# Attention over the prompt with the keys on partitions: one inversion of all softmax sums, and the division moved to GpSimd in the output projection

## The chip, the cores and the metric

The kernel runs as one program on one NeuronCore of a Trainium2 chip. The metric is the device time of one execution in microseconds, the median of several runs. The engines are TensorE (PE, with its weight loads as PEld), VectorE (DVE), ScalarE (ACT), GpSimd (POOL) and the DMA queues, the most of them fed by SyncE (SP).

## What is computed

One encoder layer for 1024 prompt tokens (8 tiles of 128 rows) and 128 sample tokens (a ninth tile). The part that the change touches is the token mixer's attention over the prompt, 8 heads, chunk-causal with chunks of 64, and what follows it:

```
proj = x @ w_in                       # cq, ckv, kr, gates gb, gc, gv
q  = rms(cq) @ w_uq                   # 8 heads x (64 + 32 rotary)
kv = rms(ckv) @ w_ukv                 # 8 heads x (64 key + 64 value)
s  = (qn.kn + qr.kr) * 96**-0.5, masked where key chunk > query chunk
p  = softmax(s);  attn = p @ v
y  = concat(attn, gb * conv3(gc * gv)) @ w_out
x  = layer_norm(alpha * x + y)        # then cross attention, LN, experts, LN
```

The sample tokens attend over a cache of 512 latents each, cross attention and a routed layer of 32 experts follow for all nine tiles.

## The kernel before

The five engines run hand-written programs side by side, each in its own order, and hand over by semaphores. PSUM is four tiles of two banks each, T[0], T[1], M[0], M[1] (128 x 1024 f32). Matrix products that must be exact but cheap use operands split in a rounded high part (ACT casts to fp32r, "high") and a low part (the difference, `take_low`, line 1629, on DVE), and three products of such parts. Others use plain f32 operands, for which the trace shows two matmul records each.

**Stages, in order of time.** Memory keys and values; the projections of nine tiles (lines 734 to 775); the attention over the prompt (PE lines 778 to 828); the attention of the sample tokens over the cache (PE lines 831 to 903, eight batches); the output projection with the first layer norm (PE lines 906 to 956, called "projection with w_out" here); cross attention; routing and experts.

**The prompt attention.** The values of all heads are eight f32 products (L782), copied out by ACT (L1333). Then per head: eight transposes turn the queries (L791), ACT copies them out with the scale (L1337); two f32 products give the keys (L795), DVE copies them (L1698). Then for eight query tiles, in the order ORDER = (2, 4, 6, 7, 5, 3, 1, 0), with the queries on partitions: scores in f32 (L806), DVE writes the mask (L1704) and takes the row maximum (L1706), ACT takes exp with the row sum accumulated (L1341), PE transposes the probabilities (L689), DVE copies them (L1719), PE multiplies them with the values in f32, 64 columns at a time (L816), and DVE scales the 128x64 result by the inverse of the row sum (L1721, L1713). SP loads each head's queries and key weights two heads ahead (L495, L496).

**The cache attention.** PE transposes the sample queries and the weights (L835, L838); ACT scales the first into qTs (L1346), DVE copies the second (L1731). Eight batches follow, and in each of them ACT and DVE split one 128-row chunk of w_out (L1376, L1629). ACT waits for all chunks of w_out (line 1366, `win_lo_in`) before the first batch's exp (L1370). GpSimd begins the convolution of tiles 0 to 3 in this stage.

**The projection with w_out.** For each tile t: GpSimd has the convolution's rows (`convolve`, lines 2143 to 2158: three multiplications in one group L2151, then L2154, L2156, L2158, all 128x512); PE turns the eight 128-column chunks of attention and convolution (`turn_mix`, L918); ACT casts the turned rows to the high part (L1388); DVE takes the low part (`mix_low`, L1770); PE runs 48 matmuls of 128x512 (L911); DVE adds the residual and takes mean and variance (`add_first`: L1755, L1757, L1758, L1761); GpSimd gives the inverse deviation (`deviation`: L2119, L2121); DVE normalises (`norm_rows`: L1765, L1768); SP stores the rows. The orders that matter, each engine's own:

```
DVE:  mix_low(0); for t in 0..7: mix_low(t+1), norm_rows(t-1), add_first(t)
POOL: convolve(0..3); for t in 0..7: deviation(t), convolve(t+4)
PE:   turn_mix(0); for t in 0..8: turn_mix(t+1), product(t)
```

ACT issues the 25 loads of the sample tile's convolution behind its cast of tile 5 (L1393, L1394). SP loads tile t's convolution inputs (`load_conv`, L519) with two buffers, and the residual rows (`load_x`, L528).

## Time and profile before

| | us |
|---|---|
| median of 3 runs | 1743.56 |
| lowest, highest | 1738.17, 1748.22 |
| profiled execution, its own time | 1737.2 |
| its span in the trace | 1735.4 |
| PE busy in the span | 1612.0 (93%) |
| DVE, ACT, POOL busy | 993.6, 751.8, 249.4 |
| mean granted TensorE clock | 0.976 |

Busy time of PE is the union of matmul records, and these overlap: a record of 128x512 lasts longer than the distance to the next. In a timeline a line stands for one instruction or for several of a kind, with its start, its length, and in brackets the idle time before it and who ended that.

### The profile page before, as it was taken

The numbers are of one execution on the slowest core, as the hardware profiler recorded it, in microseconds if no ns is written. First come the engines' busy times: TensorE is split into PE (matmuls) and PEld (weight loads), VectorE is DVE, ScalarE is ACT, GpSimd is POOL, SyncE is SP. The second block draws the span as 40 slices with busy tenths as digits, with TensorE's granted clock in tenths as the row PEclk, the third lists the DMA queues.
The fourth block names the chain that finished last, engine by engine and source line by source line (L and its number), as shares of the span: only waits on it lengthen the run. The fifth ranks groups of instructions, "written<-read, shape, count | busy, mean of one in ns | idle before, by whom it ended". The sixth has DMA issues, their size and how long they took to land.

```text
span 1735.4 us, 21728 instructions
## 1 busy us (share of the span) xinstructions
PE 1612.0 (93%) x8282; PEld 1292.7 (74%) x8282; DVE 993.6 (57%) x1347; ACT 751.8 (43%) x1062; POOL 249.4 (14%) x210
## 2 busy tenths in 40 slices
PE   8999999799998899999999998999999999999966
PEld 4578877466766688999877777788888888888852
DVE  1410111366665456422344447889988889889936
ACT  2311111332335202222332113588778778788834
POOL 0000000000007173000021110111111121111104
PEclk9999999999999999999999897999999999999988
DMA  9510111700002354300054445799999999999967
GB/s 356 216 62 29 61 53 47 240 20 20 10 12 98 146 192 172 134 25 13 22 184 149 143 136 216 258 376 379 379 383 387 376 389 385 390 383 377 363 231 299
DMA packets 134295, 351.77 MB, mean 203 GB/s; under 512 B 24498, under 2 KB 27186, under 8 KB 128708
## 3 DMA queue, kind: packets, MB, share of 16 engines
q1 hardware_dynamic: 124084, 330.69, 51.6%
q0 software_dynamic: 9216, 18.89, 2.8%
q10 hardware_dynamic: 912, 1.05, 0.2%
q8 instruction: 56, 0.92, 0.2%
q14 instruction: 27, 0.22, 0.0%
HBM read 322.19 MB, written 43.15 MB: 211 GB/s over the span
## 4 chain that ended last, share of the span: by engine, by line
PE 58%; DMA 20%; DVE 13%; ACT 4%; issue 3%; SPq 1%; POOL 0%; DVEq 0%; POOLq 0%; ACTq 0%
DMA beside<-in_w_exp_up 18%; PE M L911 11%; DVE rounded L1629 10%; PE T L753 6%; PE M L744 5%; PE M L816 3%; PE T L689 3%; PE M L1159 3%; PE T L806 3%; PE M L689 2%; PE T L970 2%; ACT rounded L1517 2%; PE T L972 2%; PE T L971 2%; PE M L999 2%
## 5 line engine op out<-in xcount | busy, mean ns | idle before, releaser
L1159 PE MATMUL M<-rounded 128*128 128x512 f32 x2304 | 548.9, 395 | 11.2 <-DVE conv_w_rows L1960 5.6
L1629 DVE TENSOR_TENSOR rounded<-beside,rounded 128x1024 fp32r<-128x1024 f32 (+2 forms) x394 | 468.0, 1234 | 114.3 <-ACT rounded L1517 56.6
L1159 PEld LDWEIGHTS M<-rounded 128*128 128x128 f32 x2304 | 429.1, 189 | 105.6 <-issue 15.0
L1517 ACT CAST rounded<-beside 128x1024 fp32r<-128x1024 f32 x256 | 259.2, 1050 | 94.9 <-DMA beside<-in_w_exp_up 88.1
L911 PE MATMUL M<-rounded 128*128 128x512 f32 x864 | 216.5, 407 | 5.2 <-DVE logits L1852 2.3
L911 PEld LDWEIGHTS M<-rounded 128*128 128x128 f32 x864 | 164.9, 195 | 43.6 <-issue 7.9
L1527 ACT CAST rounded<-beside 128x1024 fp32r<-128x1024 f32 x128 | 125.3, 1048 | 19.5 <-DMA beside<-in_w_exp_down 17.2
L2201 POOL DMA_INDIRECT expert_rows<-beside,route_out x32 | 44.4, 1389 | 380.1 <-ACT beside L1558 360.6
L1341 ACT ACTIVATE arena<-T,negmax 128x384 f32<-128x384 f32 (+3 forms) x64 | 47.4, 740 | 114.6 <-DVE negmax L1706 114.6
L1629 DVE TENSOR_TENSOR rounded<-T,rounded 128x512 fp32r<-128x512 f32 (+1 forms) x82 | 81.7, 1000 | 26.2 <-ACT rounded L1401 18.2
L689 PE MATMUL T<-tables,arena 128*128 128x128 f32 x572 | 77.8, 284 | 17.3 <-DMA arena<-in_mem_prompt 6.7
L689 PEld LDWEIGHTS T<-tables,arena 128*128 128x128 f32 x572 | 68.1, 146 | 32.9 <-issue 11.5
L806 PE MATMUL T<-arena 96*128 96x384 f32 (+3 forms) x192 | 71.8, 489 | 10.8 <-issue 10.8
L816 PEld LDWEIGHTS M<-arena 128*128 128x128 f32 x576 | 71.8, 192 | 10.3 <-issue 7.7
L744 PE MATMUL M<-rounded,x_high 128*128 128x416 f32 (+1 forms) x270 | 70.4, 374 | 6.6 <-DVE x_low L1629 6.6
L970 PE MATMUL T<-rounded 128*128 128x256 f32 x256 | 73.1, 285 | 2.4 <-issue 2.4
L816 PE MATMUL M<-arena 128*128 x576 | 72.5, 271 | 0.7
L971 PE MATMUL T<-rounded 128*128 128x256 f32 x256 | 72.4, 283 | 0.0
L972 PE MATMUL T<-rounded 128*128 128x256 f32 x256 | 72.4, 283 | 0.0
L2194 POOL DMA_INDIRECT beside<-x_rows,route_tok x32 | 52.2, 1632 | 135.6 <-PE T L1200 115.3
L753 PE MATMUL T<-rounded,x_high 128*128 128x512 f32 x270 | 65.4, 394 | 0.0
L753 PEld LDWEIGHTS T<-rounded,x_high 128*128 128x128 f32 x270 | 50.7, 188 | 11.7
(302 smaller groups left out, 2107.5 us busy)
## 6 DMA issues: line engine op xcount, KB each, us to landing
beside<-in_w_exp_gate SPq DMA_DIRECT2D x64, 1024.0 KB, 8.5
beside<-in_w_exp_up SPq DMA_DIRECT2D x64, 1024.0 KB, 11.3
beside<-in_w_exp_down SPq DMA_DIRECT2D x32, 2048.0 KB, 11.6
arena<-x_rows SPq DMA_DIRECT2D x27, 512.0 KB, 4.0
x_rows<-arena SPq DMA_DIRECT2D x18, 512.0 KB, 3.0
arena<-expert_rows SPq DMA_DIRECT2D x9, 1024.0 KB, 12.8
arena<-in_x_prompt SPq DMA_DIRECT2D x16, 512.0 KB, 3.9
arena<-in_cache_mem_k SPq DMA_DIRECT2D x8, 1024.0 KB, 5.8
```

The source lines that it names most:

```text
L689: got = nc.tensor.transpose(out[:, k * P:(k + 1) * P] if width == P else out[0:width, k * P:(k + 1) * P], rows[:, k * width:(k + 1) * widt ...
L744: got = nc.tensor.matmul(M[u][:, at:at + c1 - c0], x[:, k * P:(k + 1) * P], part[k][:, c0:c1], start=(k == 0 and part is w_in_high and x i ...
L753: got = nc.tensor.matmul(T[u][:, c:c + CW], x[:, k * P:(k + 1) * P], part[k][:, GC + c:GC + c + CW], start=(k == 0 and part is w_in_high a ...
L806: got = nc.tensor.matmul(T[n % 2][:, c:c1], qT[u][0:HW, i * P:(i + 1) * P], kT[u][0:HW, c:c1], start=True, stop=True)
L816: got = nc.tensor.matmul(o, prT[n % 2][:, c, :], value[:, c, ds(h * DV, DV)], start=(c == 0), stop=(c == i))
L911: got = nc.tensor.matmul(out[:, c:c + 512], x[k], part(k)[:, c:c + 512], start=(k == 0 and x is hi and part is high), stop=(k == KT - 1 an ...
L970: nc.tensor.matmul(out, high(k)[:, d * P:(d + 1) * P], x1T[:, 0, k], start=(k == 0), stop=False)
L971: nc.tensor.matmul(out, high(k)[:, d * P:(d + 1) * P], x1T[:, 1, k], start=False, stop=False)
L1159: got = nc.tensor.matmul(out, x[xs], (high, low)[ws](w)[:, c:c + 512], start=(first and n == 0), stop=(last and n == 2))
L1517: nc.scalar.copy(high(c), w_raw[c // 4][:, c % 4, :]).then_inc(gu_high, 1)
L1527: nc.scalar.copy(high(8 + c), w_raw[2][:, c, :]).then_inc(down_high, 1)
L1629: return nc.vector.tensor_tensor(out, x, highs.bitcast(f32), ALU.subtract)
```

## The change

In the prompt attention the keys stand on the partitions of the scores, so that the probabilities come out already in the form in which they multiply the values, and their transposes go. The row maximum is needed before the exp and per column, so it becomes part of the product: a first, rougher set of scores ("lead scores": high parts alone, queries on partitions, the 12 pieces LEADS of up to 512 columns) gives each query's maximum on DVE (`largest`); it is written as a 97th column beside the query's 96 numbers, turned with them, and meets a row of ones in the keys. Scores and values are then three products of high and low parts each. The sum of the probabilities comes from ones beside the values: 64 more output rows of the same matmul. The mask is a matmul of one row. ACT takes each exp twice (f32 and rounded), GpSimd subtracts them for the low part. Scores of one head run beside lead scores of the next.

The output of the attention, attnT, is already turned, so `turn_mix` turns only the convolution's four chunks. It is not yet divided: the sums of each head go to DRAM, come back as 64 rows, are inverted once by DVE in the cache stage (b == 3), go to DRAM again, and are loaded spread over partitions, tile by tile (`load_shares`, two DMAs each, tiles 0 and 1 by SP, 2 to 7 by ACT). GpSimd multiplies attnT by them (`divide_by_sums`).

```diff
 PE, prompt attention
+            for n in range(PT * H):
+                h, j = divmod(n, PT)
+                scores(n)
+                if n > 1:
+                    weigh_values(n - 2)
+                if h + 1 < H:
+                    if j == 0:
+                        keys(h + 1)
+                    if 1 <= j <= 4:
+                        for c in range(3 * j - 3, 3 * j):
+                            lead_scores(h + 1, c)
+                    if j == 5:
+                        turn_with_max(h + 1)
+                if j == 6 and h + 2 < H:
+                    turn_queries(h + 2)
...
+            def lead_scores(h, c):
...
+                    pe.wait_ge(negmax_ready, MAXES * h + c - 1)
...
+            def scores(n):
...
+                if n > 1:
+                    pe.wait_ge(exp_done, n - 1)
...
+                for c0, c1 in by_banks(j):
+                    for m, (k, q) in enumerate(((kT_hi, qa_hi), (kT_hi, qa_lo), (kT_lo, qa_hi))):
...
 ACT, prompt attention
+            def exponentials(n):
+                j = n % PT
+                act.wait_ge(s_ps, n + 1)
+                if n > 1:
+                    act.wait_ge(p_ready, n - 1)
+                if n > 2:
+                    act.wait_ge(o_ps, n - 2)
+                nc.scalar.activation(p_raw[n % 2][:, 0:D - j * P], T[n % 2][:, j * P:], ACT.Exp)
+                nc.scalar.activation(p_hi[n % 3][:, 0:D - j * P], T[n % 2][:, j * P:], ACT.Exp).then_inc(exp_done, 1)
...
+            act.wait_ge(sums_out, 16 * H)
 DVE, prompt attention
+            for h in range(H):
+                if h + 1 < H:
+                    keys_low(h + 1)
+                if h > 0:
+                    context(h - 1, 1)
+                if h + 1 < H:
+                    for c in range(len(LEADS)):
+                        largest(h + 1, c)
+                    larger_part(h + 1)
+                context(h, 0)
+                if h + 1 < H:
+                    scaled_low(h + 1)
+            context(H - 1, 1)
 SP, after the prompt attention
+            store_sums(H - 1)
+            load_conv(0)
+            load_conv(1)
+            sp.wait_ge(sums_out, 16 * H)
+            sp.dma_start(r_sums[0:64, :], sums_dram.rearrange("h (t c) -> (h t) c", t=PT)).then_inc(sums_out, 16)
+            for k in range(4):
+                sp.dma_start(w_out_raw[k], w_out_rows[:, k, :]).then_inc(win_lo_in, 16)
...
 DVE, cache attention
+                if b == 3:
+                    dve.wait_ge(sums_out, 16 * (H + 1))
+                    nc.vector.reciprocal(r_sums[0:64, :], r_sums[0:64, :]).then_inc(o_done, 1)
 PE, turn_mix
-                if t < PT:
-                    transposes(T[u], attn[:, t, :], 4)
-                transposes(T[u][:, 512:], conv_rows[t % 4], 4).then_inc(rowsT_ps, 1)
+                transposes(T[u][:, 512:], conv_rows[t % 3], 4).then_inc(rowsT_ps, 1)
 ACT, projection with w_out
             for t in range(NT):
                 u = t % 2
-                act.wait_ge(rowsT_ps, t + 1)
+                if t < PT:
+                    act.wait_ge(o_done, 2 * H + 1 + t + 1)
+                if t + 2 < PT:
+                    load_shares(act, t + 2)
                 if t > 1:
                     act.wait_ge(product_ps, t - 1)
-                if t < PT:
-                    nc.scalar.copy(rows_hi[u], T[u][:, :]).then_inc(rows_high, 1)
+                nc.scalar.copy(rows_hi[u][:, 0:512].rearrange("p (k c) -> p k c", k=4), attnT[:, :, t * P:(t + 1) * P] if t < PT else mixTs)
+                act.wait_ge(rowsT_ps, t + 1)
+                nc.scalar.copy(rows_hi[u][:, 512:], T[u][:, 512:]).then_inc(rows_high, 1)
 DVE, mix_low
-                if t < PT:
-                    take_low(rows_lo[u], T[u][:, :], rows_hi[u]).then_inc(rows_low, 1)
...
+                k, left = (x[u][:, 0:512].rearrange("p (k c) -> p k c", k=4) for x in (rows_lo, rows_hi))
+                take_low(k, attnT[:, :, t * P:(t + 1) * P] if t < PT else mixTs, left)
+                take_low(rows_lo[u][:, 512:], T[u][:, 512:], rows_hi[u][:, 512:]).then_inc(rows_low, 1)
 POOL
+            for n in range(PT * H):
+                w, hi, lo, raw = D - (n % PT) * P, p_hi[n % 3], p_lo[n % 3], p_raw[n % 2]
+                pool.wait_ge(exp_done, n + 1)
+                nc.gpsimd.tensor_tensor(lo[:, 0:w], raw[:, 0:w], hi[:, 0:w].bitcast(f32), ALU.subtract).then_inc(p_ready, 1)
...
+            def divide_by_sums(t):
+                pool.wait_ge(share_in[t % 2], 32 * (H // 2) + 32 * (t // 2 + 1))
+                rows = attnT[:, :, t * P:(t + 1) * P]
+                nc.gpsimd.tensor_tensor(rows, rows, shares[t and 2 - t % 2], ALU.mult).then_inc(o_done, 1)
+
-            for t in range(4):
+            for t in range(3):
                 convolve(t)
+            divide_by_sums(0)
             for t in range(PT):
+                if t + 1 < PT:
+                    divide_by_sums(t + 1)
                 deviation(t, t % 2)
-                if t + 4 < NT:
-                    convolve(t + 4)
+                if t + 3 < NT:
+                    convolve(t + 3)
             deviation(PT, 0)
```

Around these: every SBUF area of the stage has a new place; the convolution's rows have three buffers instead of four, so that three tiles are convolved ahead; the first two heads' queries are loaded before the last tile's projection is stored; four of the eight chunks of w_out, the sample queries and the sample latents are loaded behind the prompt attention; the shift of the second layer norm is loaded later, and the load of w_ukv waits for the memory values' store. DVE prepares mask rows, rows of ones and zeros and the low part of the rotary keys once (memsets and two subtractions of 32x1024), and ACT copies the rotary keys twice. The DVE order of the projection with w_out stands as it was.

## Rows read from the trace of the kernel before

**Rows 1.** Busy time by engine, prompt attention and projection with w_out (columns: stretch, length, engines, clock, DMA).
```profile
329.60:525.60 196.00, 181.60 (x1146) 138.74 (x1147) 131.41 (x327) 60.33 (x135) 0.00 (x0) 1.00 0.13 40
588.38:694.40 106.02, 105.95 (x500) 88.00 (x500) 61.24 (x63) 15.40 (x17) 52.10 (x46) 1.00 0.55 200
```

**Rows 2.** Timeline, the first scores of heads 0 and 7.
```profile
329.64 1.96 PE L806 MATMUL T<-arena 96*128 96x384 f32 x6 [1.36 <-issue]
...
504.32 1.96 PE L806 MATMUL T<-arena 96*128 96x384 f32 x6 [1.35 <-issue]
```

**Rows 3.** Groups by shape, 340 to 700 us, TensorE (busy us, mean ns of one).
```profile
L911 PE MATMUL M<-rounded 128*128 128x512 f32 x432 | 100.7, 392 | 1.6 <-ACT rounded L1388 1.6
L816 PE MATMUL M<-arena 128*128 x562 | 70.9, 271 | 0.7
```

**Rows 4.** Timeline of TensorE, fp32r matmuls of 256 columns, and one head's keys.
```profile
706.16 0.28 PE L970 MATMUL T<-rounded 128*128 128x256 f32 x1
...
706.52 0.28 PE L970 MATMUL T<-rounded 128*128 128x256 f32 x1
...
351.16 1.93 PE L795 MATMUL M<-arena 128*64 128x512 f32 x4
```

**Rows 5.** Groups by shape, 340 to 700 us, DVE and ACT.
```profile
L1706 DVE TENSOR_REDUCE negmax<-T 128x1 f32<-128x512 f32 x8 | 5.5, 691 | 0.3
L1706 DVE TENSOR_REDUCE negmax<-T 128x1 f32<-128x256 f32 x8 | 3.4, 424 | 0.3
L1341 ACT ACTIVATE arena<-T,negmax 128x1024 f32<-128x1024 f32 x7 | 7.8, 1113 | 9.5 <-DVE negmax L1706 9.5
L1341 ACT ACTIVATE arena<-T,negmax 128x128 f32<-128x128 f32 x8 | 2.9, 367 | 13.2 <-DVE negmax L1706 13.2
L1353 ACT COPY arena<-T 128x512 f32<-128x512 f32 x8 | 4.6, 569 | 2.3 <-PE T L854 2.3
```

**Rows 6.** Groups by shape, GpSimd, whole span.
```profile
L2151 POOL TENSOR_TENSOR arena<-arena,conv_w_rows 128x512 f32<-128x512 f32 x27 | 42.1, 1588 | 10.3 <-DMA arena<-gate_rows 10.3
L2174 POOL TENSOR_TENSOR rounded<-beside,rounded 128x1024 fp32r<-128x1024 f32 x9 | 21.3, 2372 | 179.7 <-ACT rounded L1467 179.7
```

**Rows 7.** Timeline, hand-over of tiles in the projection with w_out.
```profile
599.65 1.22 DVE L1755 SCALAR_TENSOR_TENSOR arena<-arena,M 128x1024 f32<-128x1024 f32 x1 [10.24 <-PE M L911]
...
602.34 0.21 DVE L1761 BATCH_NORM_AGGREGATE moments<-stats 128x2 f32<-128x12 f32 x1
...
603.05 0.57 POOL L2121 TENSOR_TENSOR rstd<-moments,minus_half 128x1 f32<-128x1 f32 x1
...
614.25 1.17 DVE L1629 TENSOR_TENSOR rounded<-T,rounded 128x1024 fp32r<-128x1024 f32 x1
...
615.34 1.28 DVE L1765 SCALAR_TENSOR_TENSOR arena<-arena,moments 128x1024 f32<-128x1024 f32 x1
616.65 1.28 DVE L1768 SCALAR_TENSOR_TENSOR arena<-arena,rstd 128x1024 f32<-128x1024 f32 x1
617.77 3.83 POOL L2151 TENSOR_TENSOR arena<-arena,conv_w_rows 128x512 f32<-128x512 f32 x3 [1.97 <-DMA arena<-gate_rows]
...
624.41 1.29 POOL L2158 TENSOR_TENSOR arena<-arena 128x512 f32<-128x512 f32 x1
```

**Rows 8.** The line of the DMAs that ACT issues (ns min, median, max of one issue).
```profile
L1393 ACTq DMA_DIRECT2D arena<-u_rows_sample x24: 366/442/734, 637.2 to 648.5; - x24
```

**Rows 9.** Timeline before the first head: ACT's start, and TensorE after an idle stretch.
```profile
314.76 1.04 ACT L1330 COPY arena<-arena 32x1024 f32<-32x1024 f32 x1 [3.75 <-DMA q_rows<-arena]
...
323.91 1.94 PE L791 MATMUL M<-tables,arena 128*96 128x128 f32 x8 [5.71 <-DMA arena<-in_w_ukv]
325.78 2.50 PE L795 MATMUL M<-arena 128*64 128x512 f32 x4
```

**Rows 10.** The cache stage's first exp, and the loads of w_out (KB, us to landing).
```profile
535.70 0.70 ACT L1370 ACTIVATE arena<-M,negmax 128x528 f32<-128x528 f32 x1 [2.21 <-DVE negmax L1740]
...
below<-in_w_out SPq DMA_DIRECT2D x8, 512.0 KB, 6.7
```

More of the change, by code:

```diff
@@ new lines, in values @@
+            def values(i, dst):
+                got = nc.tensor.matmul(dst, latT[:, i * P:(i + 1) * P], w_ukv[:, :, DN:], start=True, stop=True)
+                got.then_inc(value_ps, 1)
+            VALUE_IN = [T[0][:, 512:], T[1][:, 512:], M[1][:, 0:512], M[1][:, 512:]]
+            turn_queries(0)
+            pe.wait_ge(win_lo_in, 16)
+            for i in range(4):
+                values(i, VALUE_IN[i])
+            keys(0)
+            for c in range(len(LEADS)):
+                lead_scores(0, c)
+                if c % 3 == 2:
+                    i = 4 + c // 3
+                    pe.wait_ge(value_ready, i - 3)
+                    values(i, VALUE_IN[i - 4])
@@ L1329, in _ @@
             act.wait_ge(q_rows, 2 + NT)
[L1330 to L1342 removed]
+            act.wait_ge(conv_ps, NT)
@@ L1852, in add_logits @@
                 nc.vector.tensor_tensor(logits[:, t, :], M[t % 2][:, 0:NG + NE], b_router[:, :], ALU.add).then_inc(logits_done, 1)
-            def then(ins):
-                ins.then_inc(dve_step, step.next())
-                dve.wait_ge(dve_step, step.value())
             def wide(x, *shape):
```

470 lines of the change are left out of this document (284 added, 186 removed).

## Prediction

> **What bounds the kernel now.** I read the busy time by stage first: in the prompt attention PE is busy 181.6 of 196.0 us, in the projection with w_out 105.95 of 106.0 [rows 1]. Both are TensorE's, so time is won there only by less work for PE, and lost where PE is made to wait. Then I read the timeline of one head and of one tile of the projection, for who waits for whom, and the groups by shape for prices. A head takes (504.32 - 329.64) / 7 = 24.95 us now [rows 2], a tile of the projection 106.0 / 9 = 11.78 us [rows 1].
>
> **Prices.** An fp32r matmul of 512 columns takes 100.7 / 432 = 0.233 us, one of 256 columns a third of 0.36 = 0.12 us [rows 3, 4]. For 384 columns I take 0.18, between them. For narrower ones no row shows fp32r; L816, with 64 columns and a weight load of 128, takes 70.9 / 562 = 0.126 a record [rows 3], so weights bound it: I take 0.12, also for the transposes and the mask matmuls (64 columns). The keys of a head are four records in 1.93 us [rows 4], 1.8 without the last one's tail, unchanged. A result can be read some 0.16 us after its matmul's slot (392 less 233 ns).
>
> **A head after, if PE never waits.** The causal half is 12 pieces: six of 512 columns, two of 384, two of 256, two of 128, 1.40 + 0.36 + 0.48 = 2.24 us a set. Scores are three sets, values three, lead scores one: 15.7. Sixteen masks 1.9, keys 1.8, sixteen transposes 1.9: 21.3 us. The other engines are below that. ACT: sixteen exps, from 1.11 us at 1024 columns to 0.37 at 128 [rows 5], mean 0.74: 11.8, and six copies of 512 columns at 0.57 [rows 5]: 15.2. DVE: reductions 6 x 0.69 + 2 x 0.56 + 2 x 0.42 + 2 x 0.29 [rows 5] = 6.7, and eight instructions of 512 columns at 0.69: 12.2. POOL: 4608 columns; 2.37 us at 1024 [rows 6] and 1.29 at 512 [rows 7] give 9.7 + 8 x 0.2 = 11.3.
>
> **But PE waits for the maxima.** The lead scores go through the two banks of M[0] and are issued three in a row; PE's order is strict. The third needs the first's maximum: 0.16 us, then 0.56 to 0.69 of reduction, 0.1 back, less the second's own 0.23. That is 0.60, 0.74 and 0.60 us at j = 2, 3, 4. At j = 1 it is worse: DVE stands behind the low parts of the keys and `context(h-1, 1)`, whose two copies (1.3 us) start only when the last values of the previous head are done, right before the first lead scores. With scores(0) at 0 I get: values and keys to 3.6, scores(1) and values to 5.3, first lead scores to 6.1; DVE's copies end at 6.9, the first maximum at 7.6, the third lead at 7.7: 1.6 us. The sum is 21.3 + 3.6 = **24.9, say 25.0 us a head: what it is now**. The expected gain of about 3.6 us a head goes into the maxima. ACT lags nowhere in that walk: its keys, queries and scaled copies end before PE asks.
>
> **The start.** The first scores are at 329.6 now. After, ACT starts as now at 314.76 [rows 9], since the same stores are waited for; two rotary copies take 2.0. DVE then has memsets of single rows and two 32x1024 subtractions: I take 7 us (5 to 8; no row shows a memset of one row of 1024), the low parts of four value tiles 2.9, keys 1.3, then twelve maxima with four more value tiles between them 9.9, and turning and scaling 2.8: scores at 340.8. The early load of the first heads saves the 5.7 us for which PE waits for key weights now [rows 9], but DVE sets the start, so it gives nothing. Head 0 has no predecessor to finish: 23.0. Six more at 25.0. The last head has no lead scores and is bound by ACT's two exps and GpSimd's subtraction in turns (two raw buffers): I walk it to 15.2, and 1.9 more for values and copies. The attention ends at 340.8 + 23 + 150 + 17.1 = 530.9 against 525.5: **+5.4**.
>
> **The cache stage.** ACT now waits for the last sums' store before it writes qTs, which takes their place: some 2 us behind the end, +0.6 on PE's start, since the present start waits for its own copies 2.7 us. Four chunks of w_out are loaded behind two `load_conv` and the sums: issued by 5.1 to 6.5 us after the end, landing 6.7 us later at worst [rows 10]; the first exp stands 10.2 us after the end now (535.70), so ACT loses 0 to 2.5, I take 1.5. What is queued behind it there is the whole stage. Inversion (one instruction of 64x128), its round trip through DRAM and the loads of shares 0 and 1 end 30 us before they are needed. The sample's queries and latents land under head 7, the second norm's shift and the first heads' queries under other work: nothing. The projection with w_out starts at **+7.3** (5.4 + 0.6 + 1.5, less 0.2 for transposes).
>
> **The projection with w_out is where it is lost.** DVE's order is mix_low(t+1), norm_rows(t-1), add_first(t). mix_low(t+1) needs ACT's high part, and that now needs divide_by_sums(t+1). GpSimd does this behind deviation(t-1) **and** convolve(t+2). deviation(t-1) needs the variance, the end of add_first(t-1). So from one variance V(t-1) to the next everything is in a row, and PE's product, 11.2 us, lies beside it:
> - to the end of deviation: 603.62 - 602.55 = 1.1 [rows 7];
> - convolve: 617.77 to 625.70, 7.95 [rows 7];
> - divide: 128x512 on GpSimd, 1.29 [rows 7];
> - ACT issues two DMAs first, for rows 2 to 5: 2 x 0.44 = 0.9 [rows 8];
> - two copies of 512 columns, 1.1 [rows 5];
> - mix_low in two halves, 1.25 (one of 1024 takes 1.17) [rows 7];
> - norm_rows, 615.34 to 617.93: 2.6 [rows 7];
> - add_first, 599.65 to 602.55: 2.9 [rows 7];
> - five hand-overs, 0.25.
>
> That is 19.3 us (18.4 without the DMAs) against 11.78, for six cycles (the convolutions 3 to 8 that stand in the loop): 4 x 19.3 + 2 x 18.4 = 114. Product 7 starts 11.15 + 0.1 + 2.9 + 114 - 5.5 = 122.7 us after product 0, against 7 x 11.78 = 82.5: +40.2. PE then idles about 8 us in each cycle. After 5.7 idle us the clock was below full: the keys took 2.50 instead of 1.93 and the transposes before them 1.94 instead of 1.0 [rows 4, 9]. In the cycles a slower product is hidden; before product 7 it is not: +1.5. Products 7 and 8 keep half a microsecond each from their missing transposes: -0.9. **+40.8** in this stage.
>
> GpSimd's own price has two values. Multiplications of the convolution took 1.28 us when alone (3.83 for three) and 1.59 in the mean [rows 6, 7]; with the mean the cycle would be about 1.05 longer, the stage +6. I take the lower: in the new cycle DVE waits while GpSimd convolves. The Trainium skill, "SBUF — State Buffer", section "Who interferes with whom", says that a DVE instruction with two SBUF inputs contends with a GpSimd instruction that reads SBUF. The longer multiplications here stand beside DVE's norm_rows, so the trace agrees; by that rule the convolutions run undisturbed and the sum keeps the lower price.
>
> **Sum.** +7.3 + 40.8 = +48. Everything behind (cross attention, experts, whose weight loads are released by the cross attention's end) is shifted as a whole. Against the profiled execution, 1737.2, that is 1785; that execution lies 6.4 below the median of the runs, 1743.6, to which I add the same: **1792**.
>
> **Rivals.**
> - A: the attention runs at PE's sum, 21.3 a head, because maxima are hidden after all (DVE overlaps neighbours, PE's issue runs ahead). For it: DVE is busy only half of a head. Against it: the wait on `negmax_ready` stands in PE's own queue, two leads behind. 7 x 3.6 = 25 less: 1767.
> - B, the other side: the division does not hold DVE back, and the projection stays PE's. Its place is divide(t+1) against add_first(t): it decides where GpSimd's 10.3 us (deviation, convolve, divide) no longer start at the variance, that is if divisions run a tile further ahead than their order says. For it: GpSimd's sum of 10.3 is under 11.78. Against it: the order of its loop. The stage would be 4 us shorter: 1743.6 + 7.3 - 4 = 1747, no difference; with A as well 1722, faster.
> - C: heads are slower (27 us), from fp32r matmuls of 128 columns dearer than 0.12 (12 more of them a head at up to 0.2), ACT's DMA issues, or contention: +14 and +6: 1812.
>
> **How the numbers follow.** My case 0.65 (its own range 1780 to 1804), A 0.13, C 0.10, B alone 0.05, B with A 0.07. Half a per cent, 8.7 us, is what counts as a difference. Slower: 0.65 + 0.13 + 0.10 = 0.88, same 0.05, faster 0.07. The range leaves out B (0.12) and the edges of C: 1758 (A, with 3 us less of memsets and cycles 1 us shorter) to 1815.
>
> **What would show it.** In the profile after: first scores near 341; heads 25 us apart, with four idle stretches of PE in each ended by DVE's maxima, the longest behind `context`; last context near 531; first matmul of the w_out product near 596; then products 19 us apart, PE idle some 8 us before each, ended by DVE's low part, that by ACT, that by GpSimd's division, for products 2 to 7; the ninth right behind the eighth. Products 12 us apart would make me wrong on the larger term; heads at 21 or 27 us on the smaller one.

## The result, and the profile after

| | before | after |
|---|---|---|
| median, us (four runs each) | 1741.09 | 1862.62 |
| lowest, highest | 1738.17, 1748.22 | 1855.76, 1868.28 |
| profiled execution, span | 1737.2, 1735.4 | 1859.32, 1857.5 |
| mean granted TensorE clock | 0.976 | 0.938 |

The ratio is 1.069 (95% interval 1.0636 to 1.0744). The changed kernel is slower, as forecast, but by 122 us instead of 48, and outside the range. The profile shows where: the first product with w_out starts at 669.33 instead of 588.38 [rows 1], 81 us late where 7.3 were forecast, and the projection adds 41, as forecast. Behind it both traces run equally long: 1041 us from the end of the ninth product to the end of the program.

Busy time by engine of the four stretches, columns as in [rows 1]: attention, cache stage, products 0 to 6, and from product 7 to the start of the next stage.
```profile
349.16:600.54 251.38, 237.50 (x927) 172.01 (x928) 86.26 (x151) 96.91 (x169) 90.42 (x64) 0.83 0.05 15
600.54:669.33 68.79, 52.39 (x292) 37.62 (x290) 28.36 (x44) 32.15 (x61) 26.98 (x22) 0.93 0.29 99
669.33:790.94 121.61, 92.04 (x364) 72.64 (x365) 37.40 (x49) 8.73 (x16) 59.01 (x55) 0.89 0.43 144
790.94:819.00 28.06, 25.23 (x113) 20.64 (x113) 22.03 (x24) 10.03 (x10) 3.36 (x4) 0.95 0.59 225
```

TensorE's clock in the attention was 1.00 before; now its mean is 0.83, and 0.89 in the projection. PE is busy 237.5 of 251.4 us, so the attention is still PE's: it is the same engine with dearer work, not another engine. The first scores of heads 0 and 7 in the timeline of TensorE answer to [rows 2]:

```profile
349.19 0.94 PE L878 MATMUL T<-rounded 97*128 97x512 f32 x3 [0.74 <-ACT x_high L1438]
...
580.61 0.86 PE L878 MATMUL T<-rounded 97*128 97x512 f32 x3
```

(580.61 - 349.19) / 7 = 33.1 us a head, against 24.95 before and 25.0 forecast.

**The mask matmuls.** The timeline of TensorE and of its weight loads (PEld) at full clock, three lead scores of 384, 256 and 128 columns, each with its mask (L854):

```profile
400.44 0.34 PE L852 MATMUL M<-rounded,x_high 96*128 96x384 f32 x1
...
400.71 0.18 PEld L854 LDWEIGHTS M<-x_high 1*128 1x128 f32 x1 [0.31 <-issue]
400.71 0.29 PE L854 MATMUL M<-x_high 1*128 1x64 f32 x1
400.93 0.19 PEld L852 LDWEIGHTS M<-rounded,x_high 96*128 96x128 f32 x1
400.93 0.39 PE L852 MATMUL M<-rounded,x_high 96*128 96x256 f32 x1
...
401.25 0.18 PEld L854 LDWEIGHTS M<-x_high 1*128 1x128 f32 x1
```

The mask's weight load and its matmul start at the same moment, and so do those of the next score: neither load ran ahead under a matmul. The step from the 384-column score to the next one is 0.49 us; by my prices (0.18 + 0.12) it is 0.30. If the 384 columns keep their 0.18, the mask takes 0.31 us here, at full clock. From the 256-column score to the one after it is 0.72 us for 0.24 forecast; the wait for a maximum is a part of that.

**The waits for maxima** are there, as the list of PE's waits shows (us in total, times, longest): 15.2 us, of which 12.9 lie in the attention, and once 10.1 at the start. The list leaves out idle times under 0.15 us.

```profile
PE M L1014 <- issue: 24.1, 7, 4.4
...
PE M L852 <- DVE arena L1863: 15.2, 22, 1.5
PE M L852 <- DVE rounded L1774: 10.1, 1, 10.1
```

**The projection.** One cycle in the timeline of all engines, from one variance (L1951) to the next product:

```profile
702.50 0.21 DVE L1951 BATCH_NORM_AGGREGATE moments<-stats 128x2 f32<-128x12 f32 x1 [0.15 <-DVE stats L1948]
...
702.90 0.22 POOL L2303 TENSOR_SCALAR moments<-moments 128x1 f32<-128x1 f32 x1 [9.28 <-DVE moments L1951]
...
703.75 3.81 POOL L2342 TENSOR_TENSOR arena<-arena,conv_w_rows 128x512 f32<-128x512 f32 x3
...
711.60 1.26 POOL L2358 TENSOR_TENSOR beside<-beside 128x512 f32<-128x512 f32 x1
...
712.89 1.25 ACTq L396 DMA_DIRECT2D beside<-softmax_shares  x2
714.18 0.62 ACT L1536 CAST rounded<-beside 128x512 fp32r<-128x512 f32 x1 [18.13 <-issue]
...
715.93 0.68 DVE L1774 TENSOR_TENSOR rounded<-T,rounded 128x512 fp32r<-128x512 f32 x1
...
716.71 0.76 PE L1014 MATMUL M<-rounded 128*128 128x512 f32 x1 [4.36 <-issue]
```

Deviation, convolution, division, two DMA issues, two copies, two low parts: the forecast chain in the forecast order (the second copy and the first low part are left out of the lines). The products start at 669.33, 680.65, 697.48, 716.71, 735.92, 755.13, 773.04 and 790.94: a cycle is 19.2 us, product 7 comes 121.6 us after product 0 (forecast: 19.3 and 122.7).

### The profile page after: what moved, and what is told of

Same layout as the page of the kernel before. It is cut to its first block, busy times and chain, and to the rows that moved or that the text cites. A ratio compares the mean times of both kernels' runs of the same rounds, so it can differ in the third digit from the quotient of the medians.

```text
span 1857.5 us, 20776 instructions
## 1 busy us (share of the span) xinstructions
PE 1696.0 (91%) x8058; PEld 1340.6 (72%) x8058; DVE 962.2 (52%) x1223; ACT 794.1 (43%) x1123; POOL 342.5 (18%) x284
## 4 chain that ended last, share of the span: by engine, by line
PE 55%; DMA 17%; DVE 16%; ACT 4%; POOL 3%; issue 2%; SPq 1%; ACTq 0%; DVEq 0%; POOLq 0%
DMA beside<-in_w_exp_up 15%; DVE rounded L1774 10%; PE M L1014 7%; PE T L800 5%; PE M L791 5%; PE M L892 4%; PE T L878 4%; PE M L1260 4%; PE T L736 3%; PE T L1071 2%; PE T L1073 2%; PE T L1072 2%; PE M L760 2%; ACT rounded L1664 2%; PE M L1100 2%
## 5 line engine op out<-in xcount | busy, mean ns | idle before, releaser
L1774 DVE TENSOR_TENSOR rounded<-beside,rounded 128x1024 fp32r<-128x1024 f32 (+3 forms) x404 | 476.7, 1226 | 201.0 <-ACT rounded L1538 86.4
L1260 PE MATMUL M<-rounded 128*128 128x512 f32 x2304 | 548.0, 395 | 12.0 <-DVE conv_w_rows L2144 6.6
L1260 PEld LDWEIGHTS M<-rounded 128*128 128x128 f32 x2304 | 429.3, 189 | 105.3 <-issue 14.6
L1014 PE MATMUL M<-rounded 128*128 128x512 f32 x864 | 227.6, 422 | 29.5 <-issue 24.1
L1014 PEld LDWEIGHTS M<-rounded 128*128 128x128 f32 x864 | 172.9, 205 | 72.3 <-issue 32.1
L1674 ACT CAST rounded<-beside 128x1024 fp32r<-128x1024 f32 x128 | 125.2, 1048 | 19.7 <-DMA beside<-in_w_exp_down 18.4
L2323 POOL TENSOR_TENSOR rounded<-beside,rounded 128x1024 fp32r<-128x1024 f32 (+3 forms) x64 | 90.4, 1414 | 200.0 <-ACT rounded L1462 200.0
L1461 ACT ACTIVATE beside<-T 128x1024 f32<-128x1024 f32 (+3 forms) x64 | 41.8, 652 | 132.8 <-PE T L878 72.2
L736 PE MATMUL T<-tables,arena 128*128 128x128 f32 x540 | 74.5, 285 | 24.6 <-DMA arena<-in_mem_prompt 6.7
L736 PEld LDWEIGHTS T<-tables,arena 128*128 128x128 f32 x540 | 63.7, 146 | 42.4 <-issue 10.3
L1774 DVE TENSOR_TENSOR rounded<-T,rounded 128x512 fp32r<-128x512 f32 (+2 forms) x90 | 80.7, 905 | 25.0 <-ACT rounded L1548 18.2
L1863 DVE TENSOR_REDUCE arena<-M 128x1 f32<-128x512 f32 (+1 forms) x96 | 51.3, 555 | 78.9 <-PE M L854 52.4
L878 PE MATMUL T<-rounded 97*128 97x512 f32 (+3 forms) x288 | 83.1, 402 | 0.7 <-ACT x_high L1438 0.7
L892 PE MATMUL M<-rounded 128*128 128x512 f32 (+3 forms) x288 | 82.1, 422 | 0.7 <-POOL rounded L2323 0.7
L852 PE MATMUL M<-rounded,x_high 96*128 96x512 f32 (+1 forms) x96 | 45.1, 499 | 25.6 <-DVE arena L1863 15.2
```

Source lines behind the costliest of these rows:

```text
L736: got = nc.tensor.transpose(out[:, k * P:(k + 1) * P] if width == P else out[0:width, k * P:(k + 1) * P], rows[:, k * width:(k + 1) * widt ...
L878: got = nc.tensor.matmul(T[n % 2][:, c0:c1], k[u][0:AUG, j * P:(j + 1) * P], q[u][0:AUG, c0:c1], start=(m == 0), stop=(m == 2 and c0 > j * P))
L892: got = nc.tensor.matmul(M[1][:, c0:c1], v[:, j, h // 2, at:at + 2 * DV], p[n % 3][:, c0 - j * P:c1 - j * P], start=(j == 0 and m == 0), s ...
L1014: got = nc.tensor.matmul(out[:, c:c + 512], x[k], part(k)[:, c:c + 512], start=(k == 0 and x is hi and part is high), stop=(k == KT - 1 an ...
L1260: got = nc.tensor.matmul(out, x[xs], (high, low)[ws](w)[:, c:c + 512], start=(first and n == 0), stop=(last and n == 2))
L1674: nc.scalar.copy(high(8 + c), w_raw[2][:, c, :]).then_inc(down_high, 1)
```

## The experiments

Distances between heads are (first exp of head 7 less that of head 0) / 7; "0 to 7" is the distance between the products of tiles 0 and 7. The changed kernel has 33.1 and 121.6.

**Division a tile earlier.**

```diff
             divide_by_sums(0)
+            divide_by_sums(1)
             for t in range(PT):
-                if t + 1 < PT:
-                    divide_by_sums(t + 1)
+                if t + 2 < PT:
+                    divide_by_sums(t + 2)
```

> Only the order of GpSimd in the projection with w_out is changed: the divisions of tiles 0 and 1 stand before the loop, and division t+2 ahead of deviation t. Theory (the division behind deviation and convolution is what puts everything in a row, 19.2 us from one variance to the next): products 2 to 8 come 11.3 to 12.5 us apart instead of 17.5 to 19.2, product 7 starts some 85 us after product 0 instead of 121.6, and the kernel takes 1862 - 37 = 1825 us. Rival (something else in the cycle, ACT's two DMA issues or a GpSimd slowed by contention, holds it): products stay more than 14 us apart, over 1845 us. The heads of the attention are untouched: 33.1 us apart by both.

Measured: 1839.89 us (ratio to the kernel before 1.0568, 1.053 to 1.0605); 0 to 7 in 96.1 us. The chain of the division is worth 25.5 us in this stage, 23 in the median: less than the 37 of the theory, whose chain was real but not the only one. The stage doesn't come back to 82.1, where it was before; its products are 12.1 to 14.3 us apart, the last two 16.7. PE now waits ahead of its transposes for the convolution (L2349), and GpSimd is busy 46.4 of 49.0 us in the middle of the stage (the fifth busy time of the second line below), so the rival's slowed GpSimd has a part in it:

```profile
696.69 0.66 PE L736 MATMUL T<-tables,arena 128*128 128x128 f32 x4 [2.74 <-POOL arena L2349]
```
```profile
686.85:735.85 49.00, 43.01 (x196) 34.59 (x195) 30.78 (x28) 3.32 (x6) 46.36 (x35) 1.00 0.59 189
```

**The masks: full height, left out, another row, 32 and 64 rows.** For full height the operands are 97 rows, 96 of them zero:

```diff
-        second_half, first_half, far_row = (x_high[1][HW:AUG, c0:c1] for c0, c1 in ((0, P), (P, 2 * P), (2 * P, 2 * P + 64)))
+        second_half, first_half, far_row = (masks[0:AUG, c0:c1] for c0, c1 in ((0, P), (P, 2 * P), (2 * P, 2 * P + 64)))
...
+            nc.vector.memset(masks[0:HW, :].bitcast(f32), 0.0)
```

> The masks' operands get 97 rows (96 of them zero, the last with the values), so that the mask matmuls are as high as those of the scores; the values computed are the same. Theory R (a matmul of one row between matmuls of 96 or 97 rows can't have its weights loaded ahead): a mask with the gaps around it falls from about 0.4 to about 0.12 us, 16 x 0.28 = 4.5 us a head less, heads 28 to 29 us apart, and if the clock rises with fewer gaps 26 to 27; first scores some 3 us earlier; total 1862 - 36 = 1826 us, or down to 1810 with the clock. Rival N (any 64-column matmul that closes a group costs that): heads stay 33 us apart, 1862 us.

Measured: 1808.21 us (1.0389, 1.035 to 1.0428), 54 us less, heads 25.4 us apart. The same three lead scores in this kernel's timeline:

```profile
392.86 0.34 PE L854 MATMUL M<-rounded,x_high 96*128 96x384 f32 x1
392.87 0.19 PEld L856 LDWEIGHTS M<-masks 97*128 97x128 f32 x1
393.05 0.19 PE L856 MATMUL M<-masks 97*128 97x64 f32 x1
393.05 0.19 PEld L854 LDWEIGHTS M<-rounded,x_high 96*128 96x128 f32 x1
393.08 0.36 PE L854 MATMUL M<-rounded,x_high 96*128 96x256 f32 x1
```

The mask's weights are loaded while the score runs (392.87, 0.01 after its start), and from the 384-column score to the next it takes 0.22 us instead of 0.49: more rows, less time.

```diff
-                got = nc.tensor.matmul(M[0][:, end - 64:end], first_half, far_row, start=False, stop=True)
...
-                        got = nc.tensor.matmul(T[n % 2][:, c0:c0 + 64], second_half, far_row, start=False, stop=True)
```

> The mask matmuls are left out of both kinds of scores, so the attention is over all keys within the diagonal block; all else is the same. This gives the masks' whole price. By the prediction's price of 0.12 us it would be 16 x 0.12 = 1.9 us a head, 1862 - 16 = 1846 us. By 0.4 us as the trace of the changed kernel reads: 6.4 us a head, heads 26 to 27 us apart, 1862 - 54 = 1808 us. If the low clock in the heads comes from the gaps around masks, it goes as well: heads at 24 to 25 us, about 1795 us.

Measured: 1795.49 us (1.0331, 1.0293 to 1.0368), heads 23.5 us apart; this kernel leaves the mask out, so its result is another. So a full-height mask costs (25.4 - 23.5) / 16 = 0.12 us, and a one-row mask (33.1 - 23.5) / 16 = 0.60 us, both with what they do to the clock. The seven heads from first exp to first exp, in the changed kernel, with full-height masks and without masks:

```profile
351.29:582.63 231.34, 218.16 (x828) 156.86 (x829) 82.14 (x145) 87.35 (x153) 79.15 (x56) 0.82 0.04 11
```
```profile
351.79:529.89 178.10, 159.36 (x828) 127.79 (x829) 80.28 (x145) 85.97 (x152) 79.18 (x56) 0.95 0.06 14
```
```profile
350.76:515.30 164.54, 142.65 (x716) 109.34 (x717) 79.96 (x145) 85.97 (x152) 79.21 (x56) 0.99 0.06 15
```

The clock is 0.82, 0.95 and 0.99. Some heads ran at full clock throughout, and they give the prices without it: the second head of the changed kernel and of the kernel without masks, and the fourth with full-height masks.

```profile
382.18:410.66 28.48, 26.17 (x122) 18.66 (x121) 11.78 (x21) 12.46 (x22) 11.28 (x8) 1.00 0.06 16
```
```profile
372.83:396.46 23.63, 20.27 (x106) 15.66 (x105) 11.60 (x21) 12.42 (x23) 11.32 (x8) 1.00 0.08 20
```
```profile
427.51:452.40 24.89, 21.84 (x122) 17.71 (x121) 11.62 (x21) 12.42 (x22) 11.31 (x8) 1.00 0.07 18
```

At full clock a one-row mask costs (28.5 - 23.6) / 16 = 0.31 us, as the single step above has it, and a full-height one (24.9 - 23.6) / 16 = 0.08. The other 33.1 - 28.5 = 4.6 us a head, 32 us over seven heads, are the clock. (In the changed kernel one head ran so; with masks of 32 rows, below, two did, in 28.4 and 28.5 us.) Without masks PE's waits for maxima stand free, four a head and 3.1 us a head, for 3.6 us forecast at four places:

```profile
PE M L852 <- DVE arena L1857: 21.7, 28, 1.7
```

Is it the single row, or its place at partition 96?

```diff
-        second_half, first_half, far_row = (x_high[1][HW:AUG, c0:c1] for c0, c1 in ((0, P), (P, 2 * P), (2 * P, 2 * P + 64)))
+        second_half, first_half, far_row = (masks[0:1, c0:c1] for c0, c1 in ((0, P), (P, 2 * P), (2 * P, 2 * P + 64)))
```

> The masks stay matmuls of one row, but the row is row 0 instead of row 96 of their operands. Theory R1 (the height is what counts: one row against 96 or 97): as the changed kernel, heads 33 us apart, 1862 us. Theory R2 (the place counts: a row group at 96 that overlaps the rows in use): as with masks of full height, heads 25.5 us apart, 1808 us.

Measured: 1862.61 us, heads 32.5 us apart, as theory R1 has it: the place makes no difference. The same operands with 32 rows (`masks[0:32]`) and with 64 (`masks[0:64]`), all but the first row zero:

> The masks' operands get 32 rows, 31 of them zero, from row 0, beside scores of 96 and 97 rows. If only a height of one row is bad (some special case of a single row): heads 25.5 us apart, 1808 us. If any height that differs much from that of the neighbours costs the waiting weight load: heads 33 us apart, 1862 us.

> As the run before this one, with 64 rows. If a step between 64 rows and 96 costs as one between 1 and 97 does (the keys, 64 rows high, show gaps before them in the trace too): 33 us, 1862 us. If 64 is tall enough: 25.5 us, 1808 us. In between it would be one of the two kinds of neighbours, leads (96) or scores (97), that pays.

Measured: 1863.65 us (two runs) and heads 32.1 us apart with 32 rows, 1855.08 us (1846.35 and 1863.8) and heads 33.0 with 64. Two runs each are few, but the heads agree. A weight load of 64 rows waits as that of one row does:

```profile
402.71 0.18 PEld L856 LDWEIGHTS M<-masks 64*128 64x128 f32 x1 [0.25 <-issue]
```

So a single row is nothing special. Between neighbours of 96 and 97 rows, heights 1, 32 and 64 cost the same and 97 doesn't; between 64 and 97 I have no run. (The keys, which I called 64 rows high in what I expected, are 128 rows by 64 columns, `128*64`, and say nothing of height.)

**Lead scores spaced.** At j = 2, 3, 4 one of the three goes ahead of the scores, one between scores and values, one behind.

```diff
+                if ahead:
+                    lead_scores(h + 1, 3 * j - 3)
                 scores(n)
+                if ahead:
+                    lead_scores(h + 1, 3 * j - 2)
                 if n > 1:
                     weigh_values(n - 2)
+                if ahead:
+                    lead_scores(h + 1, 3 * j - 1)
```

> At j = 2, 3, 4 of a head the three lead scores of the next head are no longer issued in a row: one stands ahead of the scores, one between scores and values, one behind the values. Theory (PE waits for DVE's maxima, some 0.6 to 0.75 us at each of three places): PE's idle time ended by the maxima falls from 15.2 us to under 5, heads 1.5 to 2.5 us closer (31 us apart), 1862 - 14 = 1848 us. Rival (the waits only change place, ACT's exp comes later by the lead score ahead of the scores): heads stay at 33 us, 1862 us within 4.

Measured: 1850.16 us (1.0612, 1.0563 to 1.0662), heads 31.3 us apart. The median fell by 12 us, with all four runs below those of the changed kernel though the two intervals overlap. The theory has the size right and the reason in part: PE's idle time ended by maxima fell from 15.2 to 10.9 us, not under 5, and its places from 22 to 10. Where the rest of the 12 us comes from is not shown; the clock of the seven heads was 0.84 for 0.82. Together with the early division and the full-height masks:

> Masks of full height, lead scores spaced, and GpSimd's division a tile ahead, all three together. If the three gains measured alone (54, 12 and 23 us) add up: 1862 - 89 = 1773 us. If the spacing gains nothing once the masks are fast: 1785 us. If it gains more, since the gaps of the maxima are then the only ones left and the clock rises with them (heads at 23 us): 1765 us.

Measured: 1779.06 us (1.0235, 1.0206 to 1.0265), heads 24.6 us apart: 84 of the 89 us.

**Why not 82 us: DVE instead of GpSimd, and the fourth row buffer.** The first edit lets DVE divide, tile t+2 behind `mix_low(t+1)`, on top of full-height masks:

```diff
+            divide_by_sums(0)
+            divide_by_sums(1)
             mix_low(0)
             for t in range(PT):
                 mix_low(t + 1)
+                if t + 2 < PT:
+                    divide_by_sums(t + 2)
```

> Masks of full height as before, and the division is done by DVE instead of GpSimd, two tiles ahead of the product that needs it (DVE is busy some 7 us of a tile's 19). Theory (GpSimd's sum of deviation, convolution and division, stretched by DVE, is what left the early division 12 to 14 us a tile): products 11.3 to 12 us apart, product 7 starts 83 to 86 us after product 0 against 123.3 with the masks alone, 1808 - 38 = 1770 us. Rival (the convolution, stretched to 11 us by a DVE that now does more, still sets the cycle): 95 us between products 0 and 7, 1782 us.

Measured: 1798.5 us (1.0336, 1.0309 to 1.0363), 0 to 7 in 98.5 us. Taking the division away from GpSimd gives nothing beyond the earlier order (96.1). The rival is near: a convolution takes up to 10.5 us here (7.95 in [rows 7]), and PE waits for it ahead of its transposes. It doesn't say why PE has to wait for a convolution at all. What the change also did, and what I had not priced, is in the list of buffers: `conv_rows` has three rows instead of four, so the convolution of tile t+3 stands behind `deviation(t)`, and PE's transposes of that tile come one product after this deviation. This run shows another thing: the division of tile 1, ahead of the first low part, waits for its shares, and product 0 starts 9.9 us behind its transposes for 3.4 in the changed kernel.

```profile
619.68 0.69 DVE L1979 TENSOR_TENSOR beside<-beside 128x512 f32<-128x512 f32 x1 [9.22 <-DMA beside<-softmax_shares]
```

With a fourth row (in the latents' place, from the cache stage's end on) `convolve(3)` moves ahead of the loop, and `convolve(t+4)` stands in it:

```diff
-        conv_rows = [area(at, CW) for at in (46848, 47360, 45824)]
+        conv_rows = [area(at, CW) for at in (46848, 47360, 45824, 45312)]
...
-                if t + 3 < NT:
-                    convolve(t + 3)
+                if t + 4 < NT:
+                    convolve(t + 4)
```

First on the early division by GpSimd:

> The early division by GpSimd of before, and the convolved rows get back the fourth buffer that the change took from them: convolve(3) stands ahead of the loop, convolve(t+4) in it. Theory (the change made two chains of one; the division's is gone with the early order, and what kept 96 instead of 83 us between products 0 and 7 is that a tile's rows are convolved only behind the deviation of the tile three before it): 84 to 88 us between products 0 and 7, total 1840 - 10 = 1830 us. Rival (GpSimd's sum, deviation, convolution stretched by DVE, division, 12 to 13.7 us a tile, is the bound): the distance stays at 94 to 97 us, 1840 us.

Measured: 1830.94 us (1.0511, 1.0469 to 1.0553), 0 to 7 in 94.3 us: by its distance the rival's case, by its total the theory's. Six of the seven steps are 11.4 to 14.0 us; product 5 comes 19.7 us after product 4, since GpSimd waits 9.15 us for the loads of a convolution's inputs, and the division stands behind that convolution, ACT's two DMA issues and copies behind the division:

```profile
728.71 3.81 POOL L2342 TENSOR_TENSOR arena<-arena,conv_w_rows 128x512 f32<-128x512 f32 x3 [9.15 <-DMA arena<-gate_rows]
...
736.52 1.27 POOL L2358 TENSOR_TENSOR beside<-beside 128x512 f32<-128x512 f32 x1
```

Then with the division by DVE (that of tile 1 now behind `mix_low(0)`) and full-height masks:

> Masks of full height, division by DVE with the one of tile 1 behind the first low part, and four convolved rows. Theory: nothing of GpSimd's stands between two products, as in the kernel before: 83 to 85 us between products 0 and 7 (98.5 with three rows), and product 0 some 5 us nearer to its transposes than with the division of tile 1 ahead of the low part: 1798 - 18 = 1780 us. Rival (contention between DVE, which now has the division, and GpSimd sets the cycle): 94 to 98 us.

Measured: 1773.75 us (1.0189, 1.0164 to 1.0214), 0 to 7 in 85.0 us, and product 0 4.3 us behind its transposes instead of 9.9. The theory holds. Products 1 to 5 follow each other 11.36 us apart, the other three steps are 13.0, 13.6 and 13.0; from TensorE's timeline:

```profile
643.59 11.18 PE L1016 MATMUL M<-rounded 128*128 128x512 f32 x48
...
654.96 11.16 PE L1016 MATMUL M<-rounded 128*128 128x512 f32 x48
```

So two chains ran through GpSimd in the changed kernel: the division behind the deviation, and the convolution behind the deviation for want of a buffer. With the first one gone the second still holds the stage at 96 to 98.5 us; the fourth row with the division left late, which would show the first one alone, was not run.

**Towards the best version.** The start (DVE takes the keys' low parts and first maxima ahead of the values' low parts and single-row memsets), w_out's chunks loaded ahead of the convolution's inputs, no masks in the lead scores, spacing, division by DVE, full-height masks:

> Masks of full height; no masks in the lead scores (the maximum is then taken over at most 64 keys more, which shifts the exponent and not the result); lead scores spaced; division by DVE; the four chunks of w_out loaded ahead of the convolution's rows and of the sums; and at the start DVE does the keys' low parts and the first maxima before the values' low parts and the single rows. From the division by DVE at about 1770: spacing -10, lead masks -8 x 8 x 0.12 = -8, start -5, loads -4: 1743 us, level with the kernel before (1740). If the clock comes back to full in the heads, 1735; if the gains overlap, 1755.

Measured: 1767.87 us (1.0167, 1.014 to 1.0193); heads 23.7 us apart, first exp 4.1 us earlier; but the division of tile 1 ahead of the first low part waits 10.3 us for its shares, which keeps product 0 back by 7.5 us, and 0 to 7 is 99.5. The 1743 us expected took the division by DVE at 1770; it had measured 1798. Mended, with four rows and ACT's copies of keys first:

> All of these together, with the last order of the division and four rows, and ACT's copies of the first keys ahead of those of the values. From 1768 us: -14 in the projection with w_out, -7 ahead of product 0, -2 at the start: 1745 us; heads 24.0 us apart as in the run before this one. It would be level with the kernel before (1740): the heads are 1 us shorter than there, and the start and the wait between the last head and the first batch give that back. If the clock rises too, 1735.

Measured: 1754.91 us (1.0069, 1.0045 to 1.0093), 0 to 7 in 85.6 us, heads 23.6. That is 10 us over the 1745 expected. Product 7 comes 25 us earlier than in the version before it, as it should (23); but from the start of product 7 to the end of the program the profiled execution took 1074.2 us, for 1060.6 in that version and 1064.9 in the kernel before the change, and why is not shown. Then without any mask matmul and the same result, two exponentials for one:

```diff
-                nc.scalar.activation(p_raw[n % 2][:, 0:D - j * P], T[n % 2][:, j * P:], ACT.Exp)
+                for into in (p_raw[n % 2], p_hi[n % 3]):
+                    nc.scalar.activation(into[0:64, 0:64], T[n % 2][0:64, j * P:j * P + 64], ACT.Exp)
+                    got = nc.scalar.activation(into[:, 64:D - j * P], T[n % 2][:, j * P + 64:], ACT.Exp)
```

> The best version so far without any mask matmul and with the same result: the quarter of each diagonal block that the mask closes is left out of both exponentials (a 64x64 exponential and one of the columns behind it in place of one), and stays zero in the buffers from the start; ACT's 25 loads of the sample's rows are split over two tiles; values 4 and 5 are computed ahead of the first lead scores, in banks that are free there. From 1755 us: masks 64 x 0.13 = -8, loads -3, start -4: 1740 us, level with the kernel before; if the clock rises with the heads' last odd matmuls gone, 1730. Rival: ACT, 16 more exponentials a head at some 0.2 us, now holds the scores' banks longer than PE's other work covers, and heads stay at 24 us: 1748 us.

Measured: 1744.87 us (1.0021, 1.0001 to 1.0042), heads 22.3 us apart, so ACT's added exponentials hold nothing back and the rival is out. 0 to 7 is 90.2 us, 4.6 more than in the version before it, so the masks and the start gave some 14 us where 12 were expected, and the split loads took a part back: product 5 waits 7.09 us, because ACT's copies of tile 5 stand behind 12 issues in its queue.

```profile
637.12 5.56 ACTq L1551 DMA_DIRECT2D arena<-u_rows_sample  x12
642.72 1.26 ACTq L395 DMA_DIRECT2D beside<-softmax_shares  x2
644.03 0.62 ACT L1544 CAST rounded<-beside 128x512 fp32r<-128x512 f32 x1 [26.58 <-issue]
```

> As the version without masks, but SyncE and not ACT issues the 25 loads of the sample's rows, behind the residual rows of tile 5. In the last run ACT's copies of tile 5 stood behind 12 of these loads and a wait, and product 5 came 7 us late. Theory: products 11.36 us apart all through but for the clock's return, 81 to 83 us between products 0 and 7 instead of 90, 1745 - 7 = 1738 us, at most level with the kernel before (1741). Rival (SyncE's next store and load, pushed back by 11 us of issues, now come late): a gap before product 6 instead, 1745 us.

Measured: 1737.64 us, ratio 0.9978 (0.9958 to 0.9998), level with the kernel before by the half per cent that counts. The 25 issues are still too late: GpSimd's last convolution waits for its inputs, and PE 6.34 us for it ahead of product 7, so 0 to 7 is 89.0 us. The median is the theory's 1738, but not by its reason: the 7 us that it was to win between products 0 and 7 are not there, and the gap is the rival's, one product further on. The profiled execution, at 1742.7 the second longest of the twelve, is no shorter than the one before (1740.1), so no trace shows where the median fell.

```profile
671.91 1.11 PE L741 MATMUL T<-tables,arena 128*128 128x128 f32 x4 [6.34 <-POOL arena L2371]
```

## Why the prediction was right in its sign and wrong in its size

| term, us | forecast | measured |
|---|---|---|
| first scores (329.6 before) | +11.2 | +19.6 |
| heads 0 to 6 (7 x 24.95 before) | -1.7 | +56.8 |
| last head (21.2 before) | -4.1 | -1.3 |
| cache stage (62.9 before) | +1.9 | +5.9 |
| projection with w_out | +40.8 | +40.9 |
| sum | +48 | +122 |

- **The first step that failed is a price: "For narrower ones no row shows fp32r ... I take 0.12, also for the transposes and the mask matmuls (64 columns)."** It was taken from 64-column matmuls of 128 rows among others of 128 rows [rows 3]. A one-row mask between scores of 96 and 97 rows costs 0.31 us at full clock: 16 x (0.31 - 0.12) x 7 = 21 of the 58.5 us by which the heads missed.
- **The second is a term put at nothing: the clock was taken as full in the heads**, since it was 1.00 in the attention before [rows 1]. It was 0.82 in the changed kernel, and that is 32 us more. With the masks gone it was 0.99, so both errors come from the same sixteen matmuls a head: together 16 x (0.60 - 0.12) x 7 = 54 us. PE is never idle long there. Why the clock fell is open: it rises to 0.95 with full-height masks, but it is 0.92 and 0.93 in two versions that have them and the spaced leads, so the waiting loads are not all of it.
- **A row of the kernel before bears on the price**, and the prediction passes over it: matmuls of 16 rows (L879, f32) behind such of 128 rows (L878). Their weight load starts with the matmul, and they take (579.43 - 579.01) / 2 = 0.21 us each, for (579.01 - 577.92) / 8 = 0.14.

```profile
577.92 1.16 PE L878 MATMUL M<-arena 128*128 128x128 f32 x8 [0.82 <-ACT arena L1359]
579.01 0.29 PEld L879 LDWEIGHTS M<-arena 16*128 16x128 f32 x2
579.01 0.48 PE L879 MATMUL M<-arena 16*128 16x128 f32 x2
579.43 0.66 PE L689 MATMUL T<-tables,arena 128*128 128x128 f32 x4
```

- **The rest of a head was right.** Without masks a head takes 23.5 us; my sum without them is 25.0 - 1.9 = 23.1. The waits for the maxima exist, at the four places, 3.1 us a head for 3.6. Rival A (they are hidden) is excluded.
- **The start**: I summed DVE's work (12 maxima and four low parts, 9.9 us) as if DVE set it. Between 326.2 and 346.7 the leads and the last four value products are a chain PE, ACT, DVE, PE, and PE runs it at the half level (0.51, first line below), behind the 10.1 us in which it waited for DVE; a value product takes 2.08 us. The clock is a second term that I left out here. The single-row memsets, 7 us with their subtractions in the forecast, took 7.3 (315.46 to 322.72):

```profile
326.20:346.90 20.70, 17.65 (x32) 8.94 (x33) 9.74 (x23) 3.18 (x9) 0.00 (x0) 0.51 0.15 59
```
```profile
316.03 0.91 DVE L1847 MEMSET rounded<- 1x1024 f32 x1 [0.16 <-issue]
...
338.41 2.08 PE L897 MATMUL M<-arena 128*128 128x512 f32 x2
```

- **The last head** was walked to 17.1 us and took 19.9, with its eight masks.
- **The cache stage** starts late as described; ACT stands longer than the 0 to 2.5 us of the bound, its first exp is 14.3 us behind the attention's end instead of 10.2, and it is the loads of w_out that it waits for; they take 9.6 us from issue to landing in the median, for 6.7 in [rows 10]:

```profile
614.88 0.70 ACT L1516 ACTIVATE arena<-M,negmax 128x528 f32<-128x528 f32 x1 [6.73 <-DMA below<-in_w_out]
```

- **The shares** do not end "30 us before they are needed": those of tile 0 land at 645.7, 21 us ahead of ACT's copy, those of tile 1 at 674.4, 6 us ahead of product 1. That cost nothing here, since nothing of product 0 waits for them, but 6.5 and 7.5 us in the two versions that divide tile 1 first.
- **The projection** was right in chain, cycle and sum ("about 1.05 longer" should be 3 x (1.59 - 1.28) = 0.93, but enters no sum). What I did not see is that a second chain, the three row buffers, stood beneath it: rival B's price (4 us less than before once the division is early) is refuted by the early division, which left 96.1 us against 82.1.
- **The range** bounded the price of twelve other matmuls (0.2, rival C), but neither that of the masks nor the clock. The mask's measured 0.31 alone would have lifted its upper end by 21 us, to 1836; it takes the clock as well to reach 1862. The sign, to which 0.88 was given, did not depend on the error: the projection's +40.9 alone is slower.

The convolution ran at the lower price while DVE waited: the nine tiles' three multiplications took 1.33 us in the mean in the changed kernel and 1.56 once the division came early and DVE worked beside them, additions up to 2.15 instead of 1.29.

```profile
L2342 POOL TENSOR_TENSOR arena<-arena,conv_w_rows 128x512 f32<-128x512 f32 x27 | 35.1, 1328 | 5.5 <-DMA arena<-gate_rows 5.5
```
```profile
L2342 POOL TENSOR_TENSOR arena<-arena,conv_w_rows 128x512 f32<-128x512 f32 x27 | 41.4, 1563 | 6.0 <-DMA arena<-gate_rows 6.0
```

In the second run a multiplication took 2.27 us beside a normalisation by DVE (689.04) and 1.29 with DVE idle (739.41). The Trainium skill, "SBUF — State Buffer", section "Who interferes with whom", says that a DVE instruction with two SBUF inputs contends with a GpSimd instruction that reads SBUF; the two runs agree.

## What to carry to other kernels

Price a small matmul by its neighbours: in this kernel one of 1 to 64 rows among such of 96 and 97 cost five times the same one padded with zero rows, its effect on the clock included, and four times at full clock. Give the clock of a stage a term of its own when the stage's work changes: here it was the larger half of the miss. When an operation is put into an in-order engine's loop, look for every buffer that the same change took away, since two chains through one engine hide each other and cutting one shows only part. Where a price has no row of its own, the range has to reach to the dearest row of its kind, times its count.

## What the runs showed of the hardware

- A weight load of 1, 32 or 64 rows between loads of 96 and 97 rows is not overlapped with the matmul ahead, nor is the next one; at 97 rows it is. Per mask 0.31 us against 0.08 at full clock, 0.60 against 0.12 with the clock included, and the row's place makes no difference (heads 33.1 and 32.5 us apart). The Trainium skill, "TensorE: Matmul & The Clock Gate", section "Step-by-step: what each phase is for", has weight loads pulled ahead of running matmuls when their row groups don't conflict or they go to the background buffer; which of the two decides here, no run shows.
- It isn't any change of height: without masks the load of 128 rows behind scores of 97 rows starts 0.12 us before its matmul, under the score (392.31 and 392.43).
- The mean clock of seven heads was 0.82 in a kernel in which PE was busy 94% of them, and 0.99 with the masks gone. Why it falls is not settled by these runs. After PE had waited 10.1 us at the start it was 0.51 for the next 20.7 us.
- A memset of one row of 1024 elements takes DVE 0.91 us, and the one reciprocal of 64x128 0.93 us.
